# Sums of a norm's squares as one column per 128 tokens, and the gated mixer's value transposes ahead of its mixing products

## The chip, the core and the metric

The kernel runs on one core of a Trainium2 chip, as one program without collectives. The metric is the device time of one execution in microseconds (us), the median of the runs shown. The engines are TensorE (PE in the rows; PEld is its weight load), VectorE (DVE), ScalarE (ACT), GpSimd (POOL) and SyncE (SP), which issues most of the DMAs. A "bank" is one of the eight banks of PSUM, 128 partitions x 512 numbers.

## The reference, cut to what matters

Two transformer blocks run one behind the other on 512 tokens of width 1024: a state-space mixer and an RWKV mixer with a gated feed-forward part, then a block with three mixers (a gated MLP with spatial mixing, gated linear attention, sparse attention) and a routed expert part. Every norm has this form, over the channels of one token:

```python
def rms_norm(x, g):
    xf = x.astype(jnp.float32)
    y = xf * lax.rsqrt(jnp.mean(xf * xf, axis=-1, keepdims=True) + EPS)
    return (y * g.astype(jnp.float32)).astype(x.dtype)
```

It stands behind the first mixers (`post_mix_norm`), ahead of the feed-forward part (`pre_ffn_norm`), behind it (`post_ffn_norm`) and ahead of the second block's mixer (`g_norm1`). The state-space mixer has the same norm in two groups of 256 channels, and the gated MLP has the variance of a layer norm over 512 channels. The spatial mixing and the first use of the values of the gated linear attention:

```python
    mixed = jnp.einsum('gts,bcsgd->bctgd', w, vc) + b_s.T[:, :, None]
    return u * mixed.reshape(bsz, s, D_BRANCH)
...
        attn = jnp.einsum('bthd,bhsd,bhtsd->bhts', qc, kc, decay)
        o = o_inter + jnp.einsum('bhts,bhse->bhte', attn, vc)
```

## The kernel before

Activations lie with channels on the partitions and the 512 tokens (`T`) on the free axis, as tiles of 128 channels x 512 tokens in float32; `NT` = 4 is the number of 128-token pieces. The matrix products with weights are split into three, high x high, low x high and high x low parts, which ScalarE, VectorE and GpSimd prepare. There is no planner: each engine's queue is written out by hand, and semaphores order them against each other. `open_` waits until a bank is free and takes it, `close` says that it is full, `filled` and `emptied` are the waits of the readers for the one and for the other. All products go through the helper `mm` (line 453), all transposes through `tr` (line 457), ScalarE's work through `f` (line 1370), VectorE's through `tt` (1777), `ts` (1780) and `stt` (1783), so that most rows of the profile carry these lines. In a row of a product the name of the moving operand stands first and that of the loaded one second, and the tile given as 128*32 is the loaded operand's: 128 rows, 32 columns. A product of two float32 operands appears as two records.

A norm goes like this. ScalarE or VectorE makes the square of a tile. `token_sums` (line 487; `sums` calls it, and `ssd_sums` for the two groups of the state-space mixer) adds up over the channels of all tiles: for each tile four products, the loaded operand 32 columns of ones, the moving one 128 tokens of squares, and the four products go to the four strips of 32 partitions in one bank. So the sums stand as 128 partitions x 128 numbers, 32 equal rows for each piece of 128 tokens. VectorE scales them and takes the reciprocal (`invert_variance`, line 1785), ScalarE takes the root (`rstd`, line 1372), both on 128x128. `spread_rs` (line 497) copies the result to all partitions as 128x512, by four products with a column of the identity as loaded operand and the root as moving one. VectorE multiplies by it. The calls are: `sum_ssd0` and `sum_ssd1`, `sum_post_mix` and `sum_pre_ffn` (8 tiles each) behind the mixers of the first block, `sum_post_ffn` and `sum_1` behind its feed-forward part, and `gmlp_var` (4 tiles) among the second block's projections. The RWKV mixer's `head_sums` has products of its own and shares only the reciprocal and the root. Two other places in the kernel have related forms: `kk_sums` in `prepare` (line 634) loads 128 columns of squares and moves two columns of ones and zeros, and the very first norm takes the root on 128x4 (`x_rs`, line 1838) and spreads it from there.

Behind the norms `sum_post_mix` and `sum_pre_ffn`, and `sum_post_ffn` and `sum_1`, stand `last_rows`, products that make the rows of a modulation. Between the norms of a pair VectorE adds the normed tile to the residual, ScalarE squares the residual, and TensorE takes it into the next sum, tile by tile.

The gated mixer stands at the end of the second block's first projections, on TensorE's queue in this order: 16 transposes of the gated MLP's values (`gmlp_vt`, banks 4 to 7), the 16 pairs of mixing products (`mixed`, banks 4 to 7; they wait until ScalarE has evicted the transposes), 16 transposes of the linear attention's values (`gla_vt`, banks 4 to 7; ScalarE waits for the last of them, `filled(act, "gla_vt", 3)`, and evicts all four), and then eight levels of `attn` products (banks 0 to 3), each followed by one projection tile (`next_tile`, banks 5 and 6) and four short sums into `sum_qk` in bank 7. `sum_qk` is opened ahead of level 0. At each level VectorE merges the products by a mask into the attention (`merge_level`) and makes the decayed operands of the next level, for which TensorE waits (`level_ready`).

## Time and profile before

| | us |
|---|---|
| median of 3 runs | 1776.35 |
| lowest and highest run | 1770.55, 1780.47 |
| the profiled execution's own time | 1771.74 |
| its span in the profile | 1769.9 |
| TensorE busy | 1682.1 (95%) |
| its weight loads busy | 1297.7 (73%) |
| VectorE busy | 1205.4 (68%) |
| GpSimd busy | 674.3 (38%) |
| ScalarE busy | 481.5 (27%) |
| mean granted TensorE clock | 0.98 of 2.4 GHz |

Busy time is an average over stages that are bound by different things, and matrix products are pipelined with their ends modelled, so a busy TensorE is not one at its peak. What a pause or a new piece of work costs is read from the stage: which wait ends last there. The granted clock has two levels, 1.00 (2.4 GHz) and 0.50 (1.2 GHz); a value between them in a stretch is a mean over both.

### The profile page before, as it was taken

Reading aid. Unit: us, or ns where it says so; the run is one execution under the profiler, and the core shown is the slowest. Engines: PE = TensorE matmul, PEld = TensorE weight load, DVE = VectorE, ACT = ScalarE, POOL = GpSimd, SP = SyncE. Lnnn points to the kernel's source line nnn. Section 1 sums busy time; section 2 is a strip of 40 time slices with the busy share of each in tenths; the row PEclk is TensorE's granted clock in tenths of the full one; section 3 lists DMA queues with packets and bytes.
Section 4 is the critical chain, followed back from the end, with each engine's and each line's share of the span. In section 5 each row is a group of like instructions: output and inputs, shape, how many; then the busy total and the mean of one; then the engine's idle time right before and its main releaser. Section 6 shows DMA issues by size and latency. Waiting matters only on the chain.

```text
span 1769.9 us, 29184 instructions
## 1 busy us (share of the span) xinstructions
PE 1682.1 (95%) x11954; PEld 1297.7 (73%) x11954; DVE 1205.4 (68%) x1601; ACT 481.5 (27%) x740; POOL 674.3 (38%) x382
## 2 busy tenths in 40 slices
PE   7999988889899999999889999999999998999998
PEld 5887667777577777777668788788788776766665
DVE  6949676656488888888767169387654626666764
ACT  4122434422221010101231122221231024444452
POOL 4665000021446666666446534336445650000000
PEclk9999989999899999999999999999999999999999
DMA  6222431130242222222322221213212245888884
GB/s 248 96 96 96 148 122 69 51 122 25 96 170 81 95 95 95 95 91 85 109 72 95 72 66 55 72 48 116 87 53 82 86 189 203 318 350 320 349 333 159
DMA packets 34070, 230.53 MB, mean 130 GB/s; under 512 B 4132, under 2 KB 4388, under 8 KB 8232
## 3 DMA queue, kind: packets, MB, share of 16 engines
q1 hardware_dynamic: 30240, 214.48, 33.4%
q10 hardware_dynamic: 2136, 10.24, 1.5%
q0 software_dynamic: 1584, 4.21, 0.7%
q8 instruction: 86, 1.41, 0.3%
q14 instruction: 24, 0.20, 0.0%
HBM read 220.98 MB, written 9.50 MB: 130 GB/s over the span
## 4 chain that ended last, share of the span: by engine, by line
PE 80%; DVE 11%; ACT 3%; DMA 3%; issue 2%; POOL 1%; SPq 0%; DVEq 0%; POOLq 0%; ACTq 0%
PE psum L453 79%; DVE arena L1783 3%; DVE arena L1777 3%; DMA arena<-units 2%; ACT arena L1370 2%; PE psum L457 1%; DVE arena L1780 1%; DVE expert_lo L1777 1%; DMA normed<-units 1%; ACT expert_hi L1370 1%; DVE residual L1777 0%; DMA arena<-x 0%; DVE arena L2442 0%; DVE smalls L2437 0%; ACT L1370 0%
## 5 line engine op out<-in xcount | busy, mean ns | idle before, releaser
L1370 ACT ACTIVATE arena<-psum 128x512 f32<-128x512 f32 (+3 forms) x298 | 150.6, 521 | 808.0 <-PE psum L453 739.5
L453 PE MATMUL psum<-arena 64*64 64x64 f32 (+6 forms) x2852 | 219.7, 263 | 22.2 <-DVE arena L1777 11.3
L453 PEld LDWEIGHTS psum<-arena 64*64 64x64 f32 (+4 forms) x2852 | 147.9, 148 | 79.4 <-issue 50.7
L453 PE MATMUL psum<-normed_hi,w_in_hi 128*128 128x512 f32 x496 | 198.6, 400 | 4.7 <-DVE in_lo L1777 4.7
L453 PE MATMUL psum<-normed_hi,w_in_lo 128*128 128x512 f32 x496 | 196.8, 397 | 0.0
L453 PE MATMUL psum<-in_lo,w_in_hi 128*128 128x512 f32 x496 | 195.3, 394 | 0.0
L1783 DVE SCALAR_TENSOR_TENSOR arena<-arena,fixed_data 128x512 f32<-128x512 f32 x138 | 184.6, 1339 | 11.7 <-DVE arena L1780 0.2
L1777 DVE TENSOR_TENSOR arena<-arena,psum 128x512 f32<-128x512 f32 (+2 forms) x200 | 110.5, 588 | 101.4 <-PE psum L453 67.1
L2672 POOL TENSOR_TENSOR w_ff_lo<-weight_ring,w_ff_hi 128x1024 fp32r<-128x1024 f32 x65 | 165.7, 2549 | 5.4
L2672 POOL TENSOR_TENSOR w_in_lo<-weight_ring,w_in_hi 128x1024 fp32r<-128x1024 f32 x62 | 156.7, 2528 | 5.2
L2670 POOL TENSOR_SCALAR w_in_hi<-weight_ring 128x1024 fp32r<-128x1024 f32 x62 | 71.2, 1148 | 200.2 <-PE psum L453 177.5
L453 PE MATMUL psum<-in_ff_lo,w_ff_hi 128*128 128x512 f32 x344 | 137.0, 398 | 0.0
L453 PE MATMUL psum<-normed_hi,w_ff_lo 128*128 128x512 f32 x344 | 136.8, 398 | 0.0
L453 PE MATMUL psum<-normed_hi,w_ff_hi 128*128 128x512 f32 x344 | 135.2, 393 | 0.0
L2670 POOL TENSOR_SCALAR w_ff_hi<-weight_ring 128x1024 fp32r<-128x1024 f32 x65 | 73.0, 1123 | 161.9 <-PE psum L453 150.5
L1777 DVE TENSOR_TENSOR arena<-arena 128x512 f32<-128x512 f32 (+2 forms) x138 | 115.7, 843 | 7.3 <-PE psum L453 3.0
L453 PEld LDWEIGHTS psum<-normed_hi,w_in_hi 128*128 128x128 f32 x496 | 93.7, 189 | 30.6 <-issue 5.4
L2750 POOL DMA_INDIRECT out<-arena x7 | 6.8, 978 | 277.9 <-DVE arena L1777 277.9
L453 PEld LDWEIGHTS psum<-in_lo,w_in_hi 128*128 128x128 f32 x496 | 94.0, 189 | 21.4
L453 PEld LDWEIGHTS psum<-normed_hi,w_in_lo 128*128 128x128 f32 x496 | 93.8, 189 | 20.6 <-issue 0.5
L2723 POOL TENSOR_SCALAR w_out_hi<-weight_ring 128x1024 fp32r<-128x1024 f32 x8 | 10.7, 1331 | 256.4 <-PE psum L453 256.4
L1777 DVE TENSOR_TENSOR expert_lo<-arena,expert_hi 128x2048 fp32r<-128x2048 f32 x36 | 82.2, 2292 | 36.4 <-ACT expert_hi L1370 36.4
(285 smaller groups left out, 3577.0 us busy)
## 6 DMA issues: line engine op xcount, KB each, us to landing
weight_ring<-units SPq DMA_DIRECT2D x124, 1024.0 KB, 4.9
arena<-units SPq DMA_DIRECT2D x55, 1024.0 KB, 7.7
normed<-units SPq DMA_DIRECT2D x20, 1024.0 KB, 7.9
slots<-arena ACTq DMA_DIRECT2D x7, 516.0 KB, 9.1
arena<-slots SPq DMA_DIRECT2D x7, 516.0 KB, 5.8
fixed_data<-fixed ACTq DMA_DIRECT2D x1, 2944.0 KB, 9.8
arena<-x SPq DMA_DIRECT2D x4, 512.0 KB, 6.3
arena<-bias_rows ACTq DMA_DIRECT2D x2, 896.0 KB, 4.5
```

Of the source, the lines that this page charges most:

```text
L453: return nc.tensor.matmul(o, l, r, start=start, stop=stop)
L457: return nc.tensor.transpose(o, i, C("ident", k, 0, k))
L1370: return nc.scalar.activation(o, i, func, **kw)
L1777: return V.tensor_tensor(o, a, b, op)
L1780: return V.tensor_scalar(o, a, s1, s2, op0) if op1 is None else V.tensor_scalar(o, a, s1, s2, op0, op1)
L1783: return V.scalar_tensor_tensor(o, a, s1, b, op0, op1)
L2670: first = nc.gpsimd.tensor_scalar(hi, raw, 1.0, 1.0, ALU.mult, ALU.mult)
L2672: nc.gpsimd.tensor_tensor(lo, raw, hi.bitcast(F32), ALU.subtract).then_inc(sem("split_ready"), 1)
L2723: ch.link(nc.gpsimd.tensor_scalar(hi, raw, 1.0, 1.0, ALU.mult, ALU.mult))
L2750: nc.gpsimd.indirect_dma_start(out[:, :], bass.IndirectOffsetOnAxis(ap=xb[b % 3][:, D + 4:D + 5].bitcast(I32), axis=0), xb[b % 3][:, 0:D], ...
```

## The change

`token_sums` swaps its operands. For each tile there are four products again, but the loaded operand is 128 tokens of squares (128 columns) and the moving one a single column of ones, and the result is one column of the bank for each piece of 128 tokens: the sums stand as 128 partitions x 4 numbers, a token on each partition. The scaling, the reciprocal and the root are done on 128x4 (`n=NT`), only `head_sums` keeps 128x128. `spread_rs` now loads the root's column, repeated over 128 columns, and moves the identity. In the gated mixer the `gla_vt` transposes stand ahead of the wait for the `gmlp_vt` evictions and take banks 0 to 3, and `sum_qk` is opened behind the first `next_tile`. The diff:

```diff
@@ -489,9 +489,9 @@
                 o = open_(what, 0, b)
                 for k, src in enumerate(srcs):
                     pe.wait_ge(*ready(k))
-                    for j in range(4):
-                        last = mm(o[32 * j:32 * j + 32, 0:P], C("ones", P, 0, 32), src[:, j * P:(j + 1) * P],
-                                  k == 0, k == len(srcs) - 1)
+                    for t in range(NT):
+                        last = mm(o[:, t:t + 1], src[:, t * P:(t + 1) * P], C("ones", P, 0, 1), k == t == 0,
+                                  k == len(srcs) - 1 and t == NT - 1)
                 close(last, what)
 
             def spread_rs(what, b=4):
@@ -499,8 +499,8 @@
                 n_rs[0] += 1
                 pe.wait_ge(sem("rstd_ready"), n_rs[0])
                 o = open_(("rs", what), 0, b)
-                for j in range(4):
-                    last = mm(o[:, j * P:(j + 1) * P], C("ident", P, 32 * j, 32 * j + 1).to_broadcast([P, P]), v_rs[:, 0:P])
+                for t in range(NT):
+                    last = mm(o[:, t * P:(t + 1) * P], v_rs[:, t:t + 1].to_broadcast([P, P]), C("ident"))
                 close(last, ("rs", what))
 
             def tile_of(w, nk, width, col, rhs, o, first, ready=None):
@@ -1044,6 +1044,11 @@
                 for k in range(4):
                     last = tr(o[:, k * P:(k + 1) * P], p2(AV + k)[:, t * P:(t + 1) * P])
                 close(last, "gmlp_vt", t)
+            for t in range(NT):
+                o = open_("gla_vt", t, t)
+                for k in range(4):
+                    last = tr(o[:, k * P:(k + 1) * P], p2(GV + k)[:, t * P:(t + 1) * P])
+                close(last, "gla_vt", t)
             emptied(pe, "w_s")
             for t in range(NT):
                 emptied(pe, "gmlp_vt", t)
@@ -1054,11 +1059,6 @@
                     mm(o[:, c], A(g_VT, 2048)[:, t * T + g * P:t * T + (g + 1) * P], A(g_WS)[:, g * P:(g + 1) * P], True, False)
                     last = mm(o[:, c], C("ones"), M("b_s")[:, g * P:(g + 1) * P], False, True)
                 close(last, "mixed", g)
-            for t in range(NT):
-                o = open_("gla_vt", t, 4 + t)
-                for k in range(4):
-                    last = tr(o[:, k * P:(k + 1) * P], p2(GV + k)[:, t * P:(t + 1) * P])
-                close(last, "gla_vt", t)
             def row_sums(o, i, n, tile):
 
                 for j in range(4):
@@ -1072,7 +1072,6 @@
                 close(tile_of(w, KT, P, 0, in2, o, True), "p2", t)
 
             pe.wait_ge(sem("one_hot_ready"), 1)
-            sum_qk = open_("sum_qk", 0, 7)
             for lv in range(8):
                 for m in range(2):
                     pe.wait_ge(sem("level_ready"), 2 * lv + m + 1)
@@ -1086,6 +1085,8 @@
                             if t == NT - 1:
                                 close(last, ("attn", lv), 2 * m + e)
                 next_tile(24 + lv)
+                if lv == 0:
+                    sum_qk = open_("sum_qk", 0, 7)
                 pe.wait_ge(sem("sq_qk"), lv + 1)
                 last = row_sums(sum_qk, lv, 8, sq_qk)
                 if lv < 7:
@@ -1369,11 +1370,11 @@
             def f(o, i, func, **kw):
                 return nc.scalar.activation(o, i, func, **kw)
 
-            def rstd():
+            def rstd(n=NT):
 
                 n_rstd[0] += 1
                 act.wait_ge(sem("variance_inverted"), n_rstd[0])
-                f(v_rs[:, 0:P], v_tmp[:, 0:P], ACT.Sqrt).then_inc(sem("rstd_ready"), 1)
+                f(v_rs[:, 0:n], v_tmp[:, 0:n], ACT.Sqrt).then_inc(sem("rstd_ready"), 1)
 
             n_x, n_hi = [0], [0]
 
@@ -1537,7 +1538,7 @@
 
                 emptied(act, f"sum_y{m}")
                 f(proj(KK_ + m), ew(m), ACT.Square).then_inc(sem("sq_y"), 1)
-            rstd()
+            rstd(P)
             for m in range(4):
                 act.wait_ge(sem("y_joined"), m + 1)
                 f(y1.hi(4 + m), y1.raw(4 + m), ACT.Copy).then_inc(sem("y_rounded"), 1)
@@ -1782,17 +1783,17 @@
             def stt(o, a, s1, b, op0, op1):
                 return V.scalar_tensor_tensor(o, a, s1, b, op0, op1)
 
-            def invert_variance(what, scale, add, op1=ALU.add, k=0):
+            def invert_variance(what, scale, add, n=NT):
 
                 n_rstd[0] += 1
-                filled(dve, what, k)
-                V.tensor_scalar(v_tmp[:, 0:P], PSB[bank_of(what, k)][:, 0:P], scale, add, ALU.mult, op1).then_inc(freed(what, k), 1)
-                emptied(dve, what, k)
-                V.reciprocal(v_tmp[:, 0:P], v_tmp[:, 0:P]).then_inc(sem("variance_inverted"), 1)
-
-            def rstd(what, scale, add, op1=ALU.add, k=0):
-
-                invert_variance(what, scale, add, op1, k)
+                filled(dve, what)
+                V.tensor_scalar(v_tmp[:, 0:n], PSB[bank_of(what)][:, 0:n], scale, add, ALU.mult, ALU.add).then_inc(freed(what), 1)
+                emptied(dve, what)
+                V.reciprocal(v_tmp[:, 0:n], v_tmp[:, 0:n]).then_inc(sem("variance_inverted"), 1)
+
+            def rstd(what, scale, add):
+
+                invert_variance(what, scale, add)
                 filled(dve, ("rs", what))
                 return PSB[bank_of(("rs", what))]
 
@@ -2121,7 +2122,7 @@
 
             gated_y(0)
             gated_y(1)
-            invert_variance("head_sums", 1.0 / CH, 64e-5)
+            invert_variance("head_sums", 1.0 / CH, 64e-5, P)
             gated_y(2)
             link(stt(proj(RR + 3), ew(3), S("ln_w", 3), gate_of(3), ALU.mult, ALU.mult))
             for m in range(5):
```

In the rows below the name of the loaded operand stands second, and the shape is that of the result's rows x the moving columns. On TensorE, the end of the first block's mixers, `sum_post_mix` up to the first sum of `sum_pre_ffn`, of before and then of after (six of the eight tiles' rows left out):

```order
L453 MATMUL psum<-y_lo,w_out_hi 128x512
L453 MATMUL psum<-arena,fixed_data 32x128 [waits sq_post_mix,bank4_free]
L453 MATMUL psum<-arena,fixed_data 32x128 x3
...
L453 MATMUL psum<-arena,fixed_data 32x128 [waits sq_post_mix]
L453 MATMUL psum<-arena,fixed_data 32x128 x3
L453 MATMUL psum<-tiny,fixed_data 128x128 [waits bank4_free,rstd_ready]
L453 MATMUL psum<-tiny,fixed_data 128x128 x3
L453 MATMUL psum<-weight_ring,smalls 32x256 [waits bank5_free,weights1_loaded]
L453 MATMUL psum<-weight_ring,smalls 32x256 x7
L453 MATMUL psum<-arena,fixed_data 32x128 [waits sq_pre_ffn,bank0_free]
```

```order
L453 MATMUL psum<-y_lo,w_out_hi 128x512
L453 MATMUL psum<-fixed_data,arena 128x1 [waits sq_post_mix,bank4_free]
L453 MATMUL psum<-fixed_data,arena 128x1 x3
...
L453 MATMUL psum<-fixed_data,arena 128x1 [waits sq_post_mix]
L453 MATMUL psum<-fixed_data,arena 128x1 x3
L453 MATMUL psum<-fixed_data,tiny 128x128 [waits bank4_free,rstd_ready]
L453 MATMUL psum<-fixed_data,tiny 128x128 x3
L453 MATMUL psum<-weight_ring,smalls 32x256 [waits bank5_free,weights1_loaded]
L453 MATMUL psum<-weight_ring,smalls 32x256 x7
L453 MATMUL psum<-fixed_data,arena 128x1 [waits sq_pre_ffn,bank0_free]
```

The waits and their order are the same; in each sum and in the spreading the loaded and the moving operand have changed places, and a sum moves one column instead of 128.

On VectorE, the same place: the last square, the scaling and the reciprocal of `sum_post_mix`, and the first products with the spread root, before and after.

```order
L1777 TENSOR_TENSOR arena<-normed 128x512 [waits bank3_free]
L1789 TENSOR_SCALAR tiny<-psum 128x128 [waits bank4_full]
L1791 RECIPROCAL tiny<-tiny 128x128 [waits bank4_free]
L1783 SCALAR_TENSOR_TENSOR normed<-normed,fixed_data,psum 128x512 [waits bank4_full]
L1783 SCALAR_TENSOR_TENSOR normed<-normed,fixed_data,psum 128x512
```

```order
L1778 TENSOR_TENSOR arena<-normed 128x512 [waits bank3_free]
L1790 TENSOR_SCALAR tiny<-psum 128x4 [waits bank4_full]
L1792 RECIPROCAL tiny<-tiny 128x4 [waits bank4_free]
L1784 SCALAR_TENSOR_TENSOR normed<-normed,fixed_data,psum 128x512 [waits bank4_full]
L1784 SCALAR_TENSOR_TENSOR normed<-normed,fixed_data,psum 128x512
```

The two steps take 4 columns instead of 128; their waits stay.

On TensorE, the gated mixer, from the transposes of the gated MLP's values (`psum<-fixed_data,arena`, line 457) to the first `attn` products, before:

```order
L457 MATMUL psum<-fixed_data,arena 128x128 [waits bank7_free]
L457 MATMUL psum<-fixed_data,arena 128x128 x3
L453 MATMUL psum<-arena 128x128 [waits bank6_free,bank7_free,bank5_free,bank4_free]
L453 MATMUL psum<-fixed_data 128x128
...
L453 MATMUL psum<-fixed_data 128x128
L457 MATMUL psum<-fixed_data,arena 128x128 [waits bank4_free]
L457 MATMUL psum<-fixed_data,arena 128x128 x3
...
L457 MATMUL psum<-fixed_data,arena 128x128 [waits bank7_free]
L457 MATMUL psum<-fixed_data,arena 128x128 x3
L453 MATMUL psum<-arena 128x128 [waits bank0_free,level_ready,bank1_free,bank7_free,one_hot_ready]
L453 MATMUL psum<-arena 128x128 x7
L453 MATMUL psum<-arena 128x128 [waits bank3_free,bank2_free,level_ready]
```

and after:

```order
L457 MATMUL psum<-fixed_data,arena 128x128 [waits bank7_free]
L457 MATMUL psum<-fixed_data,arena 128x128 x3
L457 MATMUL psum<-fixed_data,arena 128x128 [waits bank0_free]
L457 MATMUL psum<-fixed_data,arena 128x128 x3
L457 MATMUL psum<-fixed_data,arena 128x128 [waits bank1_free]
L457 MATMUL psum<-fixed_data,arena 128x128 x3
...
L453 MATMUL psum<-arena 128x128 [waits bank6_free,bank7_free,bank5_free,bank4_free]
L453 MATMUL psum<-fixed_data 128x128
...
L453 MATMUL psum<-fixed_data 128x128
L453 MATMUL psum<-arena 128x128 [waits bank0_free,bank1_free,level_ready,one_hot_ready]
L453 MATMUL psum<-arena 128x128 x7
L453 MATMUL psum<-arena 128x128 [waits bank3_free,bank2_free,level_ready]
```

The second set of transposes now stands ahead of the first mixing product, which waits for banks 4 to 7, and takes banks 0 to 3; the first `attn` product follows the last mixing product and no longer waits for bank 7.

## Rows read from the trace of the kernel before

**Rows 1.** Page, part 4: the chain that ended last, by engine.

```profile
PE 80%; DVE 11%; ACT 3%; DMA 3%; issue 2%; POOL 1%; SPq 0%; DVEq 0%; POOLq 0%; ACTq 0%
```

**Rows 2.** Timeline, norms 1 and 2: start us, us, engine, line, operation, operands, shape, count.

```profile
465.54 2.23 PE L453 MATMUL psum<-arena,fixed_data 128*32 128x128 f32 x64
...
467.83 0.29 DVE L1789 TENSOR_SCALAR tiny<-psum 128x128 f32<-128x128 f32 x1 [0.55 <-PE psum L453]
...
469.50 1.16 PE L453 MATMUL psum<-tiny,fixed_data 128*128 128x128 f32 x8 [1.74 <-ACT tiny L1370]
...
473.51 0.66 PE L453 MATMUL psum<-arena,fixed_data 128*32 128x128 f32 x8 [1.39 <-ACT arena L1370]
...
480.98 1.26 PE L453 MATMUL psum<-arena,fixed_data 128*32 128x128 f32 x16 [0.61 <-ACT arena L1370]
...
483.98 2.07 PE L453 MATMUL psum<-tiny,fixed_data 128*128 128x128 f32 x8 [1.74 <-ACT tiny L1370]
```

**Rows 3.** Timeline, third norm and the bias rows ahead of the fourth.

```profile
871.97 1.95 PE L453 MATMUL psum<-arena,fixed_data 128*32 128x128 f32 x64
...
878.22 2.67 PE L453 MATMUL psum<-fixed_data 128*4 128x512 f32 x3
```

**Rows 4.** Timeline, TensorE: products with one, two or four moving columns.

```profile
182.15 1.94 PE L453 MATMUL psum<-arena,fixed_data 8*128 8x4 f32 x16
...
255.94 1.05 PE L453 MATMUL psum<-fixed_data,arena 128*128 128x2 f32 x8
...
259.87 1.01 PE L453 MATMUL psum<-smalls,arena 128*128 128x1 f32 x4
260.81 1.51 PE L453 MATMUL psum<-weight_ring,smalls 128*32 128x256 f32 x12
```

**Rows 5.** Groups by form: TensorE, two moving columns; busy us, mean ns of one, idle.

```profile
L453 PE MATMUL psum<-fixed_data,arena 128*128 128x2 f32 x32 | 4.1, 250 | 0.0
```

**Rows 6.** Timeline, start-up norm: reciprocal and root on 128x4.

```profile
11.09 0.18 DVE L1838 RECIPROCAL smalls<-smalls 128x4 f32<-128x4 f32 x1
...
12.67 0.20 ACT L1370 ACTIVATE smalls<-smalls 128x4 f32<-128x4 f32 x1
```

**Rows 7.** Windows: length; busy of PE, PEld, DVE, ACT, POOL; PEclk; DMA share, GB/s.

```profile
181.30:184.60 3.30, 3.30 (x28) 3.24 (x27) 1.06 (x3) 2.09 (x4) 0.00 (x0) 0.96 0.00 0
184.70:187.60 2.90, 2.90 (x8) 2.30 (x7) 0.72 (x2) 0.00 (x0) 0.00 (x0) 0.50 0.00 0
465.50:471.50 6.00, 4.20 (x89) 3.07 (x88) 3.05 (x5) 0.91 (x2) 3.71 (x2) 0.96 0.19 34
471.60:488.00 16.40, 9.65 (x96) 4.01 (x88) 12.42 (x20) 6.80 (x12) 3.39 (x2) 0.50 0.30 115
1464.60:1468.00 3.40, 3.40 (x32) 3.29 (x32) 1.96 (x11) 2.58 (x6) 0.00 (x0) 1.00 1.00 422
```

**Rows 8.** Timeline: the state-space mixer's second sum, the gated MLP's variance.

```profile
240.14 1.08 PE L453 MATMUL psum<-arena,fixed_data 128*32 128x128 f32 x16
...
1012.30 1.08 PE L453 MATMUL psum<-arena,fixed_data 128*32 128x128 f32 x32
```

**Rows 9.** Timeline, gated mixer: transposes, mixed, evictions, attn 0, memset, level 1, attn 1.

```profile
1036.31 1.91 PE L457 MATMUL psum<-fixed_data,arena 128*128 128x128 f32 x16
...
1039.31 0.46 PE L453 MATMUL psum<-arena 128*128 128x128 f32 x2 [1.09 <-ACT arena L1370]
...
1048.48 2.06 ACT L1370 ACTIVATE arena<-psum 128x512 f32<-128x512 f32 x4 [9.42 <-PE psum L457]
...
1050.64 3.20 PE L453 MATMUL psum<-arena 64*128 64x128 f32 x32 [2.20 <-issue]
...
1052.57 1.76 DVE L2318 MEMSET arena<- 128x2048 f32 x1 [3.96 <-PE psum L453]
...
1056.87 2.98 DVE L1777 TENSOR_TENSOR fixed_data<-tiny,arena 128x256 f32<-128x256 f32 x4
...
1060.27 2.06 PE L453 MATMUL psum<-fixed_data 64*128 64x128 f32 x32
```

## The prediction

> **What bounds the kernel now.** I read the chain of waits first: TensorE is 80% of the chain that ends last, VectorE 11% [rows 1]. So an edit is worth what it adds to or takes from TensorE's queue, except where TensorE itself stands waiting for a sum to go through VectorE and ScalarE. The timelines of the norms show both. After the last `w_out` product the 64 records of the first norm's sums start at once, seven of the eight squares being ready (465.54, 64 records, 2.23 us); the variance step follows at 467.83 and the spreading at 469.50 [rows 2]. The second norm is fed one square per 1.26 us by VectorE and ScalarE: its first sum starts at 473.51, the last two at 480.98, and at 482.3 they are done [rows 2]. Nothing else that TensorE could do stands between, so both pieces lie on the path. The norms behind the feed-forward part look the same: 64 records at 871.97 in 1.95 us, and then a norm that VectorE feeds square by square, with the bias rows' products ahead of its sums [rows 3]. A matrix product here is two records, so the count of records is twice that of products.
>
> **What one new sum costs.** The number of products stays: four per square before and after, eight records. What changes is the operand that is loaded. Before, 32 columns of ones are loaded and 128 columns of squares stream past, in four strips of the array; after, 128 columns of squares are loaded and one column of ones streams past. The trace has this very form, `kk_sums`: squares of the arena as the loaded operand, two moving columns. Eight such records take 1.05 us [rows 4], one alone 0.25 us [rows 5], so a step is (1.05 - 0.25)/7 = 0.114 us at the full clock. At the half clock four records with one moving column start at 259.87 and the next work at 260.81 [rows 4]: 0.235 us a step, with some change of operand in it; I take 0.225. The old form took 2.23/64 = 0.035 us or less [rows 2]. So the step is some three times dearer, and this term carries the forecast. The loads set it: the moving side is two columns only.
>
> The Trainium skill, page TensorE: Matmul & The Clock Gate, section on LDWEIGHTS, says that a load takes its column count over 1.2 in ns, whatever the rows: 107 ns for 128 columns, 27 for 32. It speaks against this change; by it the 64 records would take an estimated 6.8 us, where the rows give 7.3.
>
> **Which clock.** A stream of loads with hardly a moving column does not hold the clock. From 181.27 to 184.0 TensorE ran 8 records of `kk_sums` and then 16 with four moving columns [rows 4]. It was busy all the time, yet the clock was 0.96 over 181.30 to 184.60, so it fell to half at about 184.3, 3.1 us after that stream began, and stayed at 0.50 to 187.6 [rows 7]. In the first norm of before the same fall came 5.5 us after its sums began (0.96 over 465.50 to 471.50, then 0.50 to 488) [rows 7]. A burst of 64 new records that begins at the full clock then takes, with the fall after 3.1 us, 27 records fast and 37 slow = 11.4 us; with the fall after 5.5 us, 9.1 us. Without a fall it is 7.3, all slow 14.4. I take 10.2, the middle of the two rows.
>
> **The terms, norm by norm** (+ is slower).
> - First norm (post-mix). Sums 10.2 for 2.2: +8.0. The variance then stands in 128x4 instead of 128x128: before, 1.67 us from 467.83 to 469.50 [rows 2]; the start-up norm does the reciprocal and the root on 128x4 in 0.18 and 0.20 us [rows 6], the variance step should be no longer, and with the hand-overs it is 0.7 in all: -1.0. The spreading has as many records as before, but now meets the half clock: 2.07 instead of 1.16 [rows 2]: +0.9. Sum +7.9.
> - Second norm (pre-FFN). At the half clock eight records are 1.8 us, more than VectorE's 1.26 per square, so TensorE becomes the bound: 8 x 1.8 = 14.4 from the first sum's start, where it was 482.3 - 473.5 = 8.8 [rows 2]. +5.6 - 1.0 = +4.6. The spreading ran at half clock already.
> - Third norm (post-FFN). 10.2 for 2.0 [rows 3]: +8.2, -1.0, +0.9 for the spreading: +8.1.
> - Fourth norm. The bias rows ahead of it, 512 columns wide [rows 3], should bring the clock back, as they seem to now, so the sums start fast (0.9 us each, under 1.26, hidden); after the clock's fall some three squares are left at 1.8. That ends about 3 us later, less 1.0: +2. All hidden would be -1, all slow +6.
> - Gated mixer's variance: 32 records between projections, TensorE never waits there, 3.65 us for 1.08 [rows 8]: +2.6. Its shorter variance step is off the path.
> - The SSD norm's two sums. The second, 16 records at 240.14, meets the half clock: 3.6 for 1.08, ahead of the grams that VectorE waits for [rows 8]: +2.5, less some 0.2 of the shorter variance step behind it: +2.3. The first has as many records at the full clock: 1.8 for some 0.6, and VectorE, which waits for it, gains 0.9 behind: +0.3. If VectorE had other work through both, they would cost nothing and give up to -1.
>
> Norms together: 7.9 + 4.6 + 8.1 + 2 + 2.6 + 0.3 + 2.3 = +27.8. `head_sums` stays as it is and keeps 128x128. Registers and waits are the same in number; I cost them at nothing.
>
> **The moved transposes.** Before, TensorE stood 1.1 us ahead of `mixed` until ScalarE had emptied the four `gmlp_vt` banks, ran `mixed` from 1039.31, then the 16 `gla_vt` transposes, and stood another 2.2 us, from 1048.44 to 1050.64, since `sum_qk` opens bank 7 at once and ScalarE frees that bank last (four evictions from 1048.48) [rows 9]. That pause halved the clock: `attn` of level 0 took 3.20 us where that of level 1 took 2.06 [rows 9]. After, the transposes (1.75 us by the first 16, which take 1.91 with the last one's run) fill the first pause; `mixed` starts 0.5 us later, at 1039.8, and ends at 1047.2. `sum_qk` opens later and the transposes lie in banks 0 to 3, which ScalarE empties by about 1042.3, during `mixed`; so `attn` starts at 1047.2 instead of 1050.64: -3.4, and at the full clock 1.1 + 0.4 less for it and the tile behind it: -1.5. Who is late next? VectorE: before, it was done with `mixed` 3.96 us ahead of its memset at 1052.57, now 0.5 later, at 1049.1, so memset and merging move by 3.4; the level's products, which end at 1059.8, move to 1056.4. TensorE needs the last of them for the second half of level 1, which now starts at 1060.27 + 1.03 = 1061.3 [rows 9], 1.5 us behind; so VectorE lets TensorE keep 4.9, but not more. Bank 7 and bank 5 of the next tile are freed by VectorE's reading of `mixed`, over 2 us before they are asked for. Term: -4.9, between -3.4 and -5.5.
>
> Sum: 27.8 - 4.9 = +22.9 us. The profiled execution took 1771.7 (span 1769.9), which is 4.6 under the median of 1776.35; on the median the forecast is 1776.35 + 22.9 = 1799 us. All stages behind are paced by TensorE or start their loads when a buffer of TensorE's is done with, so I expect the delay to pass through to the end.
>
> **Rivals.**
> - *One-column streams keep the clock up.* Then the two bursts are 7.3 each (+5.1, +5.3), the second and fourth norm stay at VectorE's pace (last two sums 0.9 each instead of a shared 1.3: +0.4 each), each norm gains its 1.0, the second and fourth spreading gain 0.9 each, SSD +0.6 and mixer variance +2.6: 10.4 + 0.8 - 4.0 - 1.8 + 3.2 = +8.6; less 4.9 it is +3.7: 1780, no change that can be told. For it: no row has 128x1 for long. Against: the fall at 184.3 with TensorE fully busy.
> - *The loads overlap, and the change is faster.* If the four loads of a square went in beside one another, as the 32-column ones seem to, a record would stay at 0.035 us. Then only the savings are left: four norms at 1.0, 0.9 on SSD, 4.9 on the mixer: -9.8, 1766.5. It decides below some 0.06 us a record. Against it stand the 0.114 of `kk_sums`: same form, same engine.
> - *The moved transposes give nothing.* 32 transposes in a row could themselves let the clock fall, so that part of `mixed` runs at half clock; a half-clock stretch like that of 184.7 to 187.6 [rows 7] costs 1.5 us there, and if TensorE is still slow at `attn`, the 1.5 gained there goes too: +26, 1802. Against: in 1464.60 to 1468.00 TensorE ran nothing but transposes, and the clock was 1.00 [rows 7]. The Trainium skill, TensorE: Matmul & The Clock Gate, Part 4, says that transposes don't count as busy, which would be this rival; by that rule, the trace disagrees.
> - *The clock stays down longer.* All four norms' sums at half clock throughout (14.4 each: +4.2, 0, +4.2, +4), the SSD and mixer stretches slow for a few us more, the feed-forward part starting before the clock is back (+1.5): about +38, 1814.
>
> **How the numbers follow.** My forecast with the mix of clocks 0.62; clock kept up 0.13; overlap 0.02; moved transposes without effect 0.10; clock down longer 0.13. The forecast's own spread, from the time of the fall (9.1 to 11.4 twice), the fourth norm (-1 to +6), SSD and the mixer, is +14 to +32, 1790 to 1808. The range takes in the case of the clock kept up (1780) and the moved transposes without effect (1802), and the nearer part of the last rival: 1780 to 1811; the overlap and most of the longer half clock, 0.15 in all, are left out. A difference under 0.5% (9 us) is what a measurement of this kernel can't tell from none. Slower by more: 0.85; within: 0.13; faster: 0.02.
>
> **What would show it.** Right: the two bursts of 64 records at 8 to 12 us, with the clock at 0.50 before their end; the eight sums of the second norm in one unbroken stream of 14 us; three steps of 0.2 us in the place of 1.67; `attn` of level 0 right behind `mixed`, in 2.1 us. Wrong: a record of the new sums far from 0.11 at the full clock; the clock at 1.00 through a burst; squares that arrive after TensorE is free; a pause ahead of `attn`, or one at level 1 of more than 0.3 us for VectorE.

## The result and the profile after

The changed kernel took 1797.41 us (median of 4 runs, 1786.65 to 1802.89) and the kernel before 1773.45 (median of 4, 1769.18 to 1780.47): a ratio of 1.0117, with a 95% interval of 1.0086 to 1.0149. That is slower by some 21 us; the forecast was 1799 us and +22.9. The profiled execution took 1800.31 us (span 1798.5, mean clock 0.969), 28.6 more than the profiled one of before, so about 8 us of what the two traces differ by is not the edit's. They are found below.

TensorE's share of the chain that ends last went from 80% [rows 1] to 82%. Page of the changed kernel, part 4, first line:

```profile
PE 82%; DVE 10%; ACT 3%; DMA 3%; issue 2%; POOL 1%; DVEq 0%; SPq 0%; POOLq 0%; ACTq 0%
```

Norms 1 and 2 in the timeline of the changed kernel (start us, us, engine, line, operands, shape, count), beside [rows 2]:

```profile
473.09 8.72 PE L453 MATMUL psum<-fixed_data,arena 128*128 128x1 f32 x64
481.85 0.16 DVE L1790 TENSOR_SCALAR tiny<-psum 128x4 f32<-128x4 f32 x1 [6.93 <-PE psum L453]
482.05 0.18 DVE L1792 RECIPROCAL tiny<-tiny 128x4 f32<-128x4 f32 x1
482.26 0.21 ACT L1371 ACTIVATE tiny<-tiny 128x4 f32<-128x4 f32 x1 [8.38 <-DVE tiny L1792]
...
482.52 2.08 PE L453 MATMUL psum<-fixed_data,tiny 128*128 128x128 f32 x8 [0.70 <-ACT tiny L1371]
...
487.57 13.79 PE L453 MATMUL psum<-fixed_data,arena 128*128 128x1 f32 x64 [1.11 <-ACT arena L1371]
...
502.06 2.07 PE L453 MATMUL psum<-fixed_data,tiny 128*128 128x128 f32 x8 [0.70 <-ACT tiny L1371]
...
506.99 0.47 PE L453 MATMUL psum<-normed_hi,w_ff_first_hi 128*128 128x512 f32 x1 [1.03 <-DVE in_ff_lo L1778]
```

The burst of 64 records takes 8.72 us for 2.23, the three steps of the variance together 0.7 us for 1.67, and the second norm's sums are one unbroken stream of 13.79 us in which TensorE no longer waits for a square. Windows over the same stretch (length; busy us of PE, PEld, DVE, ACT, POOL; then PEclk, DMA share, GB/s):

```profile
473.10:477.00 3.90, 3.90 (x37) 3.90 (x36) 1.01 (x1) 0.60 (x1) 3.58 (x2) 1.00 0.02 4
477.00:481.00 4.00, 4.00 (x27) 4.00 (x27) 0.00 (x0) 0.00 (x0) 0.13 (x1) 0.69 0.73 242
481.00:482.50 1.50, 0.81 (x4) 0.72 (x4) 0.34 (x2) 0.21 (x1) 0.00 (x0) 0.50 0.13 55
482.50:506.00 23.50, 21.63 (x112) 18.48 (x112) 12.34 (x21) 6.51 (x12) 3.39 (x2) 0.50 0.12 45
506.00:508.00 2.00, 1.01 (x4) 0.86 (x5) 2.00 (x4) 1.34 (x3) 0.00 (x0) 1.00 0.04 8
```

TensorE is busy for the whole 3.90 and 4.00 us of the first two, and its clock falls from 1.00 to 0.50 all the same, at about 478.5, 5.4 us behind the burst's start (0.69 over 477 to 481). It stays there through the second norm (0.50 over 482.5 to 506). The burst's later loads and every one of the second norm's cost nearly twice as much for it (0.215 us for 0.114).

The third and fourth norm, timeline of TensorE, beside [rows 3]:

```profile
889.95 9.13 PE L453 MATMUL psum<-fixed_data,arena 128*128 128x1 f32 x64
899.88 2.08 PE L453 MATMUL psum<-fixed_data,tiny 128*128 128x128 f32 x8 [0.80 <-ACT tiny L1371]
903.60 2.65 PE L453 MATMUL psum<-fixed_data 128*4 128x512 f32 x4
906.18 11.68 PE L453 MATMUL psum<-fixed_data,arena 128*128 128x1 f32 x64
```

The gated mixer, TensorE, ScalarE and VectorE, beside [rows 9]:

```profile
1068.58 3.65 PE L457 MATMUL psum<-fixed_data,arena 128*128 128x128 f32 x32
...
1072.27 2.07 ACT L1371 ACTIVATE arena<-psum 128x512 f32<-128x512 f32 x4 [0.94 <-PE psum L457]
...
1079.31 2.06 PE L453 MATMUL psum<-arena 64*128 64x128 f32 x32
1081.67 1.76 DVE L2319 MEMSET arena<- 128x2048 f32 x1 [0.38 <-issue]
```

All 32 transposes run in one piece, the clock at 1.00 (window of the changed kernel over them and `mixed`),

```profile
1064.00:1076.00 12.00, 12.00 (x89) 11.12 (x88) 7.35 (x11) 6.27 (x11) 3.15 (x2) 1.00 0.17 70
```

and `attn` of level 0 follows `mixed` without a pause, in 2.06 us. From the first transpose to `attn` of level 1 (1087.35) it is 18.77 us, where it was 23.96 (1036.31 to 1060.27).

**The 8 us that are not the edit's.** One stretch of code that the diff leaves as it is runs at another clock in the two traces: the state-space mixer's heads from 192 to 212 us. Windows of the changed kernel, then of the kernel before:

```profile
192.00:200.00 8.00, 8.00 (x38) 4.87 (x37) 4.33 (x10) 1.56 (x4) 0.00 (x0) 0.50 0.79 264
200.00:212.00 12.00, 12.00 (x71) 7.41 (x70) 4.18 (x9) 1.88 (x4) 0.00 (x0) 0.50 0.34 98
```

```profile
192.00:200.00 8.00, 8.00 (x58) 5.39 (x58) 5.57 (x13) 2.33 (x5) 0.00 (x0) 0.79 0.75 263
200.00:212.00 12.00, 12.00 (x101) 7.58 (x100) 7.37 (x16) 3.86 (x8) 0.00 (x0) 1.00 0.67 205
```

The changed kernel leaves this stretch 7.5 us later than the kernel before, having entered it 0.4 early: 7.9 us. It is a matter of the single execution: one and the same kernel of the experiments below, profiled twice, ran it once at 0.50 and 0.56 and once at 1.00.

### The profile page after: what moved, and what is told of

It reads as the page before. It is cut to its first block, busy times and chain, and to the rows that moved or that the text cites. A ratio compares the mean times of both kernels' runs of the same rounds, so it can differ in the third digit from the quotient of the medians.

```text
span 1798.5 us, 29185 instructions
## 1 busy us (share of the span) xinstructions
PE 1726.5 (96%) x11954; PEld 1345.2 (75%) x11954; DVE 1196.8 (67%) x1601; ACT 481.2 (27%) x740; POOL 679.4 (38%) x382
## 4 chain that ended last, share of the span: by engine, by line
PE 82%; DVE 10%; ACT 3%; DMA 3%; issue 2%; POOL 1%; DVEq 0%; SPq 0%; POOLq 0%; ACTq 0%
PE psum L453 81%; DVE arena L1784 3%; DVE arena L1778 2%; DMA arena<-units 2%; PE psum L457 2%; ACT arena L1371 1%; DVE arena L1781 1%; DVE expert_lo L1778 1%; DMA normed<-units 1%; ACT expert_hi L1371 1%; DVE arena L2443 0%; DVE smalls L2438 0%; ACT L1371 0%; DVE acts_hi L1822 0%; DVE yb_lo L1778 0%
## 5 line engine op out<-in xcount | busy, mean ns | idle before, releaser
L2751 POOL DMA_INDIRECT out<-arena x7 | 10.8, 1550 | 276.2 <-DVE arena L1778 276.2
L453 PEld LDWEIGHTS psum<-normed_hi,w_in_lo 128*128 128x128 f32 x496 | 94.0, 189 | 20.7 <-issue 0.5
```

What stands on the lines that cost most here:

```text
L453: return nc.tensor.matmul(o, l, r, start=start, stop=stop)
L2751: nc.gpsimd.indirect_dma_start(out[:, :], bass.IndirectOffsetOnAxis(ap=xb[b % 3][:, D + 4:D + 5].bitcast(I32), axis=0), xb[b % 3][:, 0:D], ...
```

## The experiments

A norm's time is compared from its pair's first sum (the burst) to the first product of the next stage, which takes the sums, the variance steps, the spreading and the modulation rows between:

| kernel | norms 1 and 2, us | norms 3 and 4, us | whole, against before |
| --- | --- | --- | --- |
| before | 23.4 | 23.3 | |
| changed | 33.9 | 33.7 | 1.0117 |
| norms_only (128 loaded, 1 moving) | 35.6 | 33.7 | 1.0126 |
| wide_moving (128 loaded, 128 moving) | 26.3 | 26.5 | 1.0016 |
| halves (64, 1) | 23.9 | 24.8 | 1.000 |
| halves_in_turn (64, 1) | 25.9 | 25.9 | 0.9999 |
| wide_halves (64, 128) | 26.1 | 26.3 | 1.0018 |
| quarters2 (32, 1) | 25.0 | 24.8 | 0.9997 |
| mixer_twice (strips) | 23.4 | 23.5 | 0.9974 |
| fed_narrow2 (64, 1 in norms 2 and 4) | 23.0 | 22.9 | 0.9978 |
| fed_wide2 (64, 128 in norms 2 and 4) | 22.1 | 22.1 | 0.9962 |

All but the first and norms_only have the mixer's new order too.

**The two halves of the change apart.** In norms_only the mixer is put back; in mixer_only the mixer alone is changed.

> The changed kernel with the gated mixer's order put back: the second set of value transposes stands behind the mixing products again and sum_qk opens bank 7 ahead of level 0. Theory A (the price is the loads of 128 columns, 0.114 us a record at the full clock and about 0.215 at the half): the norms alone cost +25 us against the kernel before, so about 1798 to 1802 where the changed kernel is at 1797, and it is slower than the changed kernel by the mixer's 5 us. In its trace the pause of 2.2 us stands again ahead of attn of level 0, which takes about 3.2 us. Rival: if the mixer's order gave nothing that lasts to the end (given back later at a weight transfer), this kernel comes out the same as the changed one, at a ratio of about 1.012 to the kernel before.

> The kernel before with the gated mixer's new order alone (value transposes ahead of the mixing products, sum_qk opened behind the first tile); the norms' sums stay as they were. Theory A: -5.3 us at the mixer, as the changed kernel's trace showed there (32.4 to 27.1 us of delay), and little of it lost later: 1768 to 1769 for a kernel before at 1773.5, a ratio of 0.997. Rival: the gain is taken back at the next wait for a weight transfer, ratio 1.000. If the 16 more transposes in a row cost clock, mixed takes over 7.4 us and the gain is 3.5 us.

norms_only: 1794.18 us, ratio 1.0126 (1.0073 to 1.018). mixer_only: 1765.29 us, ratio 0.9956 (0.9929 to 0.9983), and a second time, as mixer_twice:

> The kernel before with the gated mixer's new order alone, once more, beside the three kernels below. Expected: 0.9956 to 0.997 of the kernel before, as the first time; rival (the first ratio was the chance of its runs): 1.000.

1765.16 us, 0.9974 (0.9948 to 1.0001). So the mixer's order is a gain of 5 to 8 us that lasts to the end (expected 5.3), and the norms' form a loss of about 22 (expected 25; the interval, +13 to +32, holds it). That norms_only would come out slower than the changed kernel by the mixer's 5 us isn't seen: 1.0126 and 1.0117 have intervals that cover each other, and cover the 5 us as well. Nor do the profiled executions settle it: behind the stretch from 192 to 212 us norms_only loses some 2 us more than the changed kernel, being 5 us slower over the norms and the mixer and 2.6 faster behind them. What its trace does show is that two of the places depend on when the clock falls. TensorE, timeline of norms_only, the two bursts of sums and the pause ahead of `attn`:

```profile
463.38 10.38 PE L453 MATMUL psum<-fixed_data,arena 128*128 128x1 f32 x64
...
479.51 13.79 PE L453 MATMUL psum<-fixed_data,arena 128*128 128x1 f32 x64 [1.11 <-ACT arena L1370]
...
1074.94 2.06 PE L453 MATMUL psum<-arena 64*128 64x128 f32 x32 [2.20 <-issue]
```

The same 64 records took 10.38 us here and 8.72 in the changed kernel, since the clock fell sooner: windows of norms_only, in which it goes at about 467, 3.6 us behind the start.

```profile
463.40:466.00 2.60, 2.60 (x26) 2.60 (x24) 1.00 (x1) 0.60 (x1) 2.29 (x2) 1.00 0.00 0
466.00:468.00 2.00, 2.00 (x15) 2.00 (x15) 0.00 (x0) 0.00 (x0) 1.41 (x1) 0.74 0.03 8
```

And the pause of 2.20 us is back, but this time the clock did not fall in it: `attn` of level 0 took 2.06 us, not the 3.20 of [rows 9]. From the first transpose to level 1 it is 22.37 us here and 18.77 with the new order. So 3.6 us of the mixer's gain are the pauses' in both traces of the old order, and the other 1.6 were the clock's in the one trace of before.

mixer_only and mixer_twice are the same code. Windows from 192 us, of mixer_only and then of mixer_twice:

```profile
192.00:200.00 8.00, 8.00 (x44) 4.88 (x40) 3.87 (x9) 1.50 (x3) 0.00 (x0) 0.50 0.66 247
200.00:212.00 12.00, 12.00 (x69) 7.10 (x62) 3.44 (x7) 2.06 (x5) 0.00 (x0) 0.56 0.40 123
```

```profile
192.00:200.00 8.00, 7.89 (x69) 4.86 (x69) 6.07 (x15) 3.06 (x7) 0.00 (x0) 1.00 0.85 289
200.00:212.00 12.00, 12.00 (x110) 7.66 (x112) 8.41 (x19) 3.00 (x6) 0.00 (x0) 1.00 0.69 248
```

The burst of the first norm starts at 472.78 in the one and at 460.13 in the other, and the profiled executions took 1777.66 and some 1761 us. Of the 14 profiled executions of this case, four ran the stretch near 0.50 (the changed kernel's among them), three as the kernel before (0.79, then 1.00), seven at 1.00. Over the stretch mixer_only loses 9.2 us to mixer_twice (it enters 1.4 early and leaves 7.8 late), of the 12.65 at the first norm and the 16.6 at the end. That this also makes most of the 8 to 23 us by which the other runs of one kernel differ is likely, but not shown: only one or two executions of each were profiled.

**Which of the mixer's two edits.** only_qk moves the opening of `sum_qk` alone:

```diff
-            sum_qk = open_("sum_qk", 0, 7)
             for lv in range(8):
...
                 next_tile(24 + lv)
+                if lv == 0:
+                    sum_qk = open_("sum_qk", 0, 7)
```

> The kernel before with one edit: sum_qk opens bank 7 behind the first tile's products instead of ahead of level 0; the value transposes stay behind the mixing products. Theory: the pause of 2.2 us ahead of attn of level 0 shrinks to what banks 0 to 3 ask for (none, mixed's banks 4 to 7 hold the transposes), attn of level 0 takes 2.1 us instead of 3.2: 3.3 to 3.7 us at this place, total ratio 0.998. Rival: attn of level 0 waits for ScalarE's evictions all the same, because its merged operand or its free banks come from there: gain 0.

only_vt moves the transposes alone:

> The kernel before with the other edit alone: the value transposes stand ahead of the mixing products, in banks 0 to 3, and sum_qk still opens bank 7 ahead of level 0. Theory: the first pause of 1.1 us is filled; the second now ends when VectorE has read the last mixed result out of bank 7, about 1 us behind mixed, instead of 2.2: a gain of 2 to 4 us at this place, less than both edits together (5.2). Rival: VectorE's reading of bank 7 lasts longer than ScalarE's evictions did, pause of 2 us or more, gain 1.1 us or less.

only_qk: 1767.93 us, ratio 0.9977 (0.9943 to 1.0011). only_vt: 1763.44 us, 0.9957 (0.9922 to 0.9991). In time they can't be told from each other or from both together; the traces tell them apart. TensorE, timeline of only_vt, then of only_qk: transposes, `attn` of levels 0 and 1.

```profile
1032.58 3.65 PE L457 MATMUL psum<-fixed_data,arena 128*128 128x128 f32 x32
1044.21 2.06 PE L453 MATMUL psum<-arena 64*128 64x128 f32 x32 [0.83 <-issue]
1052.24 2.06 PE L453 MATMUL psum<-fixed_data 64*128 64x128 f32 x32
```

```profile
1045.07 1.91 PE L457 MATMUL psum<-fixed_data,arena 128*128 128x128 f32 x16
1055.30 1.91 PE L457 MATMUL psum<-fixed_data,arena 128*128 128x128 f32 x16
1057.14 2.06 PE L453 MATMUL psum<-arena 64*128 64x128 f32 x32
1065.17 2.06 PE L453 MATMUL psum<-fixed_data 64*128 64x128 f32 x32
```

From the first transpose to level 1: 19.66 us with the transposes moved, where a pause of 0.83 is left ahead of `attn` (the profile names nothing that it waits for; the expectation put it to VectorE's reading of the last `mixed` result out of bank 7, and it is gone where the opening of that bank is moved too); 20.10 with the opening moved, where the pause of 1.09 ahead of `mixed` is left; 18.77 with both; 22.4 or 24.0, by the clock, with neither. Against the 24.0 of before these are gains of 4.3 and 3.9 us, a little over the 2 to 4 and the 3.3 to 3.7 expected; against the 22.4 of norms_only, in which the clock did not fall, they are 2.7 and 2.3. The transposes' move takes out the first pause and leaves 0.83 of the second's 2.20; the opening's move takes out the second and leaves the first as it was.

**What moves past the loads.** wide_moving keeps the loads of 128 columns and moves 128 columns of ones past each instead of one. (In this kernel and in wide_halves the second state-space sum fills all of its bank and writes over modulation values that are kept there, so the values behind it are not the reference's; the work is the same.)

```diff
-                        last = mm(o[:, t:t + 1], src[:, t * P:(t + 1) * P], C("ones", P, 0, 1), k == t == 0,
+                        last = mm(o[:, t * P:(t + 1) * P], src[:, t * P:(t + 1) * P], C("ones"), k == t == 0,
```

> The changed kernel, but each sum moves 128 columns of ones past the loaded squares instead of one, so that the result stands 128 times in 128 columns and the variance step takes every 128th. Same loads, same count of products, same hand-overs. Theory A (one moving column does not hold the clock, the loads set the time): the clock stays at 1.00 through the first norm's 64 records, which take 7.3 us instead of 8.7 (0.114 each), and the sums of the second norm are fed at VectorE's pace again (done about 8.9 us after the first, instead of 13.8); in all some 10 us faster than the changed kernel, 1786 to 1789. Rival B (the clock falls whatever moves, by the stall ahead or by chance): the clock falls to 0.50 in the burst here too and the times are those of the changed kernel or longer, 64 records in 8.7 us or more, the second norm in 13.8. Rival C (moving columns add to the load instead of running beside it): a record takes 0.16 us or more and the kernel is slower than the changed one.

1775.14 us, ratio 1.0016 (0.9982 to 1.005). By the ratios that is 18 us under the changed kernel (by the medians, which come from different runs of the kernel before, 22), nearly twice what was expected. TensorE, timeline of wide_moving, the sums of norms 1 and 2:

```profile
465.27 7.30 PE L453 MATMUL psum<-fixed_data,arena 128*128 128x128 f32 x64
...
477.29 9.52 PE L453 MATMUL psum<-fixed_data,arena 128*128 128x128 f32 x64 [1.85 <-ACT arena L1371]
```

and its windows:

```profile
465.30:469.00 3.70, 3.70 (x35) 3.70 (x34) 1.01 (x1) 0.60 (x1) 3.40 (x2) 1.00 0.02 4
469.00:472.60 3.60, 3.57 (x32) 3.38 (x31) 0.00 (x0) 0.00 (x0) 0.32 (x1) 1.00 0.61 182
...
477.30:482.00 4.70, 4.46 (x32) 3.83 (x32) 4.70 (x8) 2.34 (x4) 0.00 (x0) 1.00 0.47 195
482.00:487.00 5.00, 4.51 (x34) 3.80 (x32) 2.80 (x6) 2.05 (x4) 2.18 (x2) 1.00 0.00 0
```

Same loads, same count, more columns to move, and it is faster: the clock stays at 1.00 through both norms, 64 records take 7.30 us = 0.114 each, and the second norm goes at VectorE's pace. The moving columns cost nothing beside the load. So the two parts of theory A stand: the load sets the price of a record, and a stream with one moving column lets the clock fall though TensorE is busy throughout. The expectation missed by counting the sums alone, which take 9.7 us less; the spreading and the modulation rows between the norms run at the full clock as well, and the two pairs of norms together take 14.8 us less than in the changed kernel. The clock does not stay up for good: it falls for 3.4 us at the first products of the feed-forward part, behind the last window shown, and 8 of them take some 1.5 us more, which the table does not count and the changed kernel does not pay there.

**What a load costs.** halves splits each load in two:

```diff
-                        last = mm(o[:, t:t + 1], src[:, t * P:(t + 1) * P], C("ones", P, 0, 1), k == t == 0,
-                                  k == len(srcs) - 1 and t == NT - 1)
+                        for h in range(2):
+                            last = mm(o[h * CH:(h + 1) * CH, t:t + 1], src[:, t * P + h * CH:t * P + (h + 1) * CH],
+                                      C("ones", P, 0, 1), k == t == 0, k == len(srcs) - 1 and t == NT - 1)
```

> The changed kernel, but each load of 128 columns of squares is split into two of 64 columns, which write the two halves of the sum's partitions: 16 records per square instead of 8. Theory A (the cost goes by columns loaded): 0.057 us a record at the full clock, so 128 records take the same 8.7 us in the first norm (0.107 at the half clock), and the kernel is the same as the changed one within 5 us. Rival (the cost goes by record or product, some 0.11 us whatever is loaded): 128 records take 15 to 17 us, the second norm 27 us, and the kernel is over 30 us slower than the changed one. If loads of different halves of the array overlap, as those of 32 columns may do, 64 columns cost half as much again: the first norm's sums take about 4.5 us and the kernel is some 15 us faster than the changed one.

1768.78 us, ratio 1.000 (0.9968 to 1.0033), by the ratios 21 us under the changed kernel: neither of the first two theories, but the third, stronger than stated. TensorE, timeline of halves, first norm:

```profile
460.96 3.90 PE L453 MATMUL psum<-fixed_data,arena 128*64 128x1 f32 x128
```

Twice the records in less than half the time, 0.030 us a record at the clock 1.00. That breaks the count by columns: 128 columns cost 0.114 us in one load and 0.061 in two. quarters2 goes on to loads of 32 columns:

> The changed kernel with each load split into four of 32 columns (32 records a square), one moving column. Theory E1 (below 128 columns a record costs some 0.03 us whatever is loaded, a floor per record): the first norm's 256 records take 7.7 us at the full clock and the fed norms about 2 us a square at the half clock; the kernel is some 20 us slower than the one with loads of 64. Theory E2 (the cost goes by columns at 0.5 ns each, 64 in 0.030): 256 records in 3.9 us, same time as that kernel. A value between would be the form's own price.

1768.76 us, ratio 0.9997 (0.9968 to 1.0026). TensorE, timeline of quarters2, the first norm:

```profile
458.40 1.88 PE L453 MATMUL psum<-fixed_data,arena 128*32 128x1 f32 x204
462.45 0.92 PE L453 MATMUL psum<-fixed_data,arena 128*32 128x1 f32 x52 [2.17 <-issue]
```

The first 204 records take 0.009 us each, so 128 columns cost 0.037 us; there is no floor of 0.03 us a record, and neither E1 nor E2 is right. Then TensorE stands for 2.17 us with nothing but its own instructions to wait for, so the 256 records end after 4.97 us and the split is worth no more than halves; the last 52, behind the pause, ran at the clock 0.50, in 0.018 us each. That the wait is for the supply of instructions is what "issue" suggests; no run tested it.

If loads into different column parts run beside one another, two at a time for 64 and four for 32, then 128 columns should cost 0.114, 0.057 and 0.029 us, which is near the measured 0.114, 0.061 and 0.037. halves_in_turn was meant to settle that. It swaps the two inner loops, so that four products of one half stand in a row:

> The kernel with split loads (64 columns each, 0.030 us a record at the full clock where 128 columns take 0.114) in another order: within a square all four products of the lower half of the array's columns, then all four of the upper half, instead of the two halves by turns. Theory D (loads into different column parts of the array run beside one another, and that is why split loads are cheap): 8 records in a row now meet in the same half, so a record costs 0.055 us or so, the first norm's 128 records take about 7 us instead of 3.9, and the kernel is 8 to 12 us slower than the one with the halves by turns. Rival E (a load of 64 columns is cheap in itself, whatever the order): 128 records in 3.9 us again and the same time as that kernel, 1769.

1769.02 us, ratio 0.9999 (0.9971 to 1.0027). TensorE, windows of halves_in_turn in the first norm's sums:

```profile
466.20:468.00 1.80, 1.80 (x53) 1.79 (x52) 1.01 (x1) 0.60 (x1) 1.54 (x2) 1.00 0.00 0
468.00:470.00 2.00, 2.00 (x68) 2.00 (x66) 0.00 (x0) 0.00 (x0) 2.00 (x1) 1.00 0.00 0
```

121 records in 3.80 us are 0.031 each, as with the halves by turns, not 0.055; only the clock, which fell at about 470, makes the sums 4.82 us in all. Rival E holds: the order doesn't matter. Why narrow loads are cheaper for each column stays open: either they run beside one another over more than eight records, or a narrow load is cheap in itself. The Trainium skill, TensorE: Matmul & The Clock Gate, Part 3, says that loads are pulled ahead of products in flight within a window of 64, where the row groups differ or the load goes to a background buffer. These loads use all rows; by the buffer the halves could meet in either order. No run here shows it.

**Narrow loads, wide moving.** wide_halves moves 128 columns past loads of 64:

> The kernel with split loads (64 columns, halves by turns), but 128 columns of ones moved past each, so that each sum stands 128 times in every fourth column of the bank; the variance step takes the first four columns. Theory A (the moving columns hold the clock): clock 1.00 through both norms at 461 to 485 us, where the one-column form fell to 0.50 by 467. If the two halves' products also run side by side, the first norm's 128 records take 3.9 us and the kernel is 3 to 5 us faster than the one with one column (1764 to 1766); if the moving columns add up (128 columns at 2.4 GHz are 0.053 us a record), 7 us and the kernel is 2 us slower to 3 us faster than it. Rival: the clock falls after the first norm's burst as before, no gain.

1770.66 us, ratio 1.0018 (0.9982 to 1.0053). The first norm's 128 records, TensorE, timeline of wide_halves:

```profile
458.85 7.21 PE L453 MATMUL psum<-fixed_data,arena 128*64 128x128 f32 x128
```

0.056 us a record: here the moving columns set the price, and the halves' products don't run side by side. What the clock gives is lost to that, and it did not stay up throughout, as the expectation had it: it was 0.66 over 472 to 477, in the second norm's sums.

**The best of both.** Strips (the old form) are cheapest in a burst; the short variance step is worth 1 us where VectorE's pace hides dearer sums. fed_wide2 and fed_narrow2 have the mixer's order and the new sums in norms 2 and 4 alone:

> The gated mixer's new order, and the new form of sum in the two norms alone that VectorE feeds square by square (pre-FFN and the one behind the experts), with 64 loaded columns by turns and 128 moving; all other sums in strips as before. Theory A (moving columns bring the clock back, loads of 64 columns keep up with VectorE): 16 records take 0.9 us at the full clock and 1.0 to 1.8 at the half, the clock is back at 1.00 before the sums end, the spreading behind them takes 1.16 us instead of 2.07, the variance step is 1.0 shorter: 1 to 2 us less for each of the two norms, in all 2 to 4 us under the kernel with the mixer's order alone. Rival: at the half clock 16 records with 128 moving columns take 1.8 us against 1.26 for a square, TensorE falls behind by some 2 us in each norm before the clock is back, and nothing is won: same time as the mixer's order alone, or 2 us over it.

> As the kernel with 128 moving columns in the two fed norms, but with one moving column. Theory A: 16 records take 1.02 us at the half clock, under VectorE's 1.26, so all but the last two squares are hidden; the end comes 0.6 later and the variance step is 1.0 shorter: -0.4 us a norm, the clock stays at 0.50 and the spreading at 2.07. In all 1 us under the mixer's order alone, which can't be told from none. Rival: the same 2 to 4 us as with 128 moving columns, if what helps is not the clock but the short variance step.

fed_wide2: 1765.38 us, ratio 0.9962 (0.994 to 0.9984). fed_narrow2: 1766.64, 0.9978 (0.9952 to 1.0004). The first norms of fed_wide2, TensorE, timeline:

```profile
461.04 2.22 PE L453 MATMUL psum<-arena,fixed_data 128*32 128x128 f32 x64
...
469.01 9.44 PE L453 MATMUL psum<-fixed_data,arena 128*64 128x128 f32 x128 [1.32 <-ACT arena L1379]
479.17 1.16 PE L453 MATMUL psum<-fixed_data,tiny 128*128 128x128 f32 x8 [0.71 <-ACT tiny L1379]
```

The spreading took 1.16 us at the full clock instead of 2.08, and each pair of norms is 1.2 to 1.4 us shorter than with strips alone, as expected (2 to 4 in all), and 0.4 to 0.6 with one moving column. Against the whole this is within the interval of mixer_twice. What can be measured of a gain, 0.3 to 0.4%, comes from the mixer's order. The interval of fed_wide2 lies below 1, but so do those of mixer_only and only_vt, and none of these can be told from another.

## Why the prediction was right

The measured ratio, put on the median that the forecast started from (1776.35), gives 1797.1 us; the forecast was 1799. Its sign and mechanism held: a record of the new sums costs 0.114 us at the full clock and 0.215 at the half, the clock falls within the burst (5.4 us in; 3.6 in norms_only), and TensorE paces what follows. That the totals lie within 2 us of each other is in part luck: the ratio's interval is +15 to +26 us, and the terms missed by up to 2.3 us, most of them against each other. Place by place, by its own terms:

- First and second norm: +12.5 forecast, +10.5 in the changed kernel, +12.2 in norms_only. The burst was put at 10.2 us between two falls of the clock; it took 8.72 and 10.38. The stream of the second norm was put at 14.4 and took 13.79 in both: 0.215 us a record at the half clock, where 0.235 was read from four records with a change of operand in them and 0.225 taken. The variance steps took 0.7 us, the spreading 2.08, as said.
- Third and fourth: +8.1 and +2 forecast, +10.35 measured together, but split otherwise. The third's burst took 9.13 us where 10.2 was put, which makes it +7. The fourth cost some 3 us instead of 2: the bias rows' products brought the clock back only for a short time (0.84 over 905 to 910, then 0.50), and the sums took 11.68 us. The two terms were mis-sized by 1 us each, against each other.
- The first state-space sum: +0.3 forecast, +0.4 measured.
- The second state-space sum: +2.3 forecast, 0 measured. It took 1.95 us (247.55), at the full clock, for 1.08. The term rested on where the clock lay in one trace, and that is not fixed in this part of the kernel.
- The gated MLP's variance: +2.6 forecast, +4.0 measured. The records took 3.63 us as said; behind them the clock dipped (0.72 over 1044 to 1050), which the term had left out, though the argument on one-column streams should have put it there (norms_only dips there too, wide_moving does not).
- The mixer: -4.9 forecast, -5.2 between the two traces, -3.6 against norms_only, and a gain of 5 to 8 us (intervals 0 to 13) in the medians. The pauses' part was right; the 1.5 us at the full clock depended on a fall that doesn't come every time. `memset` followed with 0.38 us of waiting, and level 1 had no pause.
- Rest of the kernel: forecast nothing, measured +1.5. It is -0.85 and -1.7 where the clock of the kernel before dips and the changed one's does not (0.89 over 1165 to 1180 and 0.83 over 1470 to 1480, for 1.00), and some +4 at the experts' end. There ScalarE waited 3.74 us for a transfer of weights, where it had waited 2.10; TensorE stood 2.40 us (at 1645.95) for 0.73, and its next 8 records took 5.31 us for 3.67, with the clock fallen. In norms_only that pause was 0.87 and the 8 records took 3.67, so this is not the new sums' own price. The forecast's "I expect the delay to pass through to the end" held but for this 1.5.

The terms that are the edit's sum to 0.4 + 10.5 + 10.35 + 4.0 - 5.2 = +20 us, the medians' ratio to +20.7. The forecast's 22.9 is 3 more: 2.0 too many on the first two norms and 2.3 on the second state-space sum, 1.4 too few on the MLP. Of its rivals, wide_moving shows what "one-column streams keep the clock up" would have given: forecast +3.7 for that case, measured +2.8 (ratio 1.0016, interval -3 to +9 us) with the clock at 1.00 through all four norms. "The loads overlap" was rejected by the rows of `kk_sums` and rightly so for loads of 128 columns. "The moved transposes give nothing" fell with the window above (1.00 over all 32). For loads of 64 and 32 columns the overlap's case is nearly what was found.

## What to carry to other kernels

Which operand of a product is loaded matters more than how many columns move: a record with 128 columns of squares loaded costs 0.114 us, one with 32 columns of ones loaded and the squares moved past them in strips 0.035. A stream that loads much and moves little can halve TensorE's clock while the engine is fully busy, and the price is then paid by all that follows, so look at the granted clock behind such a stream and not at its busy share. And before building on a clock seen in one trace, look whether a second execution shows the same: here one stretch of unchanged code was worth 8 to 9 us either way.

## What was not expected of the hardware

- 128 loaded columns cost 0.114 us in one load, 0.061 in two of 64, 0.037 in four of 32, whatever the order of the halves (wide_moving, halves, quarters2, halves_in_turn). With 128 moving columns past them, two halves cost 0.113 again (wide_halves).
- 128 moving columns are free beside a load of 128 (7.30 us for 64 records) and held the clock at 1.00 through that stream (wide_moving); with one moving column the clock fell 3.6 to 5.4 us into the same stream.
- The Trainium skill's price of a load (TensorE: Matmul & The Clock Gate, section on LDWEIGHTS), columns over 1.2 in ns, is near the 0.114 us of 128 columns (107 ns) and does not agree, for loads one behind another, with 0.030 and 0.009 us for 64 and 32 columns, where it gives 53 and 27 ns.
- In quarters2, 204 records of 9 ns each were followed by 2.17 us (and, at the third norm, 201 by 2.12) in which TensorE stood and the profile names nothing that it waited for.
- The clock in the stretch from 192 to 212 us took one of three courses in each of the 14 executions, and a different one in mixer_only than in mixer_twice, which are one kernel.
